# Start bytes of the matmul operands in SBUF: fixed tile strides, and odd weight chunks 128 bytes further on

## The reference

```python
        h = h + jax.nn.sigmoid(h @ w_ple_gate[i]) * e
...
        h = _layer_norm(DEEPNORM_ALPHA * h + mix, ln_g[layer, 0], ln_b[layer, 0])
        h = _layer_norm(DEEPNORM_ALPHA * h + _sq_relu_mlp(h, ffn_w1[layer], ffn_w2[layer]),
                        ln_g[layer, 1], ln_b[layer, 1])
```

## Time and profile before

| | |
|---|---|
| time, median of three runs | 1188.33 us (1186.57 to 1188.77) |
| span of the profiled execution | 1182.6 us |
| time around the span, against the median | 5.7 us |
| PE busy | 1134.0 us, 8737 matmuls |
| DVE busy | 822.2 us |
| ACT busy | 644.3 us |
| granted TensorE clock, mean | 0.978 |
| matmuls of `three` | 7860 |

### The profile page before, as it was taken

The page is one execution under the profiler, slowest core; times in us unless marked ns, Lnnn a source line. Parts: engine busy times, 40 slices in busy tenths (PEclk is TensorE's granted clock), DMA queues, the critical chain, the costliest instruction groups (busy, mean ns, idle before and its releaser), DMA issues.

```text
span 1182.6 us, 23980 instructions
## 1 busy us (share of the span) xinstructions
PE 1134.0 (96%) x8737; PEld 1077.7 (91%) x8737; DVE 822.2 (70%) x1454; ACT 644.3 (54%) x1249; POOL 412.5 (35%) x453
## 2 busy tenths in 40 slices
PE   6987989999998999999999999999999999999997
PEld 6975779999997989869999999999979999999996
DVE  6899688888557776755788745496456567887454
ACT  5675756555645555665556534374425645665342
POOL 5886332333413101124566412200013334665130
PEclk9998999999999999978999999999999999999998
DMA  6531156667455633303555555565422555555651
GB/s 191 139 116 36 37 143 172 184 182 200 135 195 187 205 119 96 113 31 108 171 160 173 178 174 177 172 217 180 164 72 85 198 180 174 182 177 183 199 175 48
DMA packets 199371, 178.27 MB, mean 151 GB/s; under 512 B 5730, under 2 KB 197589, under 8 KB 199044
## 3 DMA queue, kind: packets, MB, share of 16 engines
q1 hardware_dynamic: 198788, 173.37, 46.8%
q0 software_dynamic: 512, 3.96, 0.9%
HBM read 176.26 MB, written 1.05 MB: 150 GB/s over the span
## 4 chain that ended last, share of the span: by engine, by line
PE 80%; DVE 10%; ACT 4%; issue 2%; POOL 2%; DMA 1%; SPq 0%; ACTq 0%; DVEq 0%; POOLq 0%
PE ps L1799 24%; PE ps L1800 23%; PE ps L1801 23%; DVE wlo L1199 3%; PE ps L2147 2%; ACT whi L706 2%; DVE cv L1280 2%; PE ps L2277 2%; POOL acc L518 1%; PE ps L2104 1%; DVE ta L1412 1%; PE ps L2129 1%; PE ps L2255 1%; DMA raw<-w_in 1%; ACT sq L721 1%
## 5 line engine op out<-in xcount | busy, mean ns | idle before, releaser
L1199 DVE TENSOR_TENSOR wlo<-raw,whi 128x1024 fp32r<-128x1024 f32 x329 | 410.2, 1284 | 166.6 <-ACT whi L706 165.1
L706 ACT ACTIVATE whi<-raw 128x1024 fp32r<-128x1024 f32 x330 | 331.8, 1050 | 177.6 <-PE ps L1801 155.9
L1799 PE MATMUL ps<-xh,whi 128*128 128x256 f32 (+2 forms) x912 | 262.5, 288 | 13.8 <-DVE xl L1217 5.5
L1800 PE MATMUL ps<-xl,whi 128*128 128x256 f32 (+2 forms) x912 | 258.7, 284 | 0.0
L1801 PE MATMUL ps<-xh,wlo 128*128 128x256 f32 (+2 forms) x912 | 258.1, 283 | 0.0
L1799 PE MATMUL ps<-xrh,whi 128*128 128x274 f32 (+2 forms) x832 | 242.3, 291 | 0.0
L1801 PE MATMUL ps<-xrh,wlo 128*128 128x274 f32 (+2 forms) x832 | 238.7, 287 | 0.0
L1800 PE MATMUL ps<-xrl,whi 128*128 128x274 f32 (+2 forms) x832 | 238.6, 287 | 0.0
L1799 PE MATMUL ps<-fh,whi 128*128 128x256 f32 (+1 forms) x688 | 194.3, 282 | 1.9 <-DVE wlo L1199 1.9
L1800 PE MATMUL ps<-fl,whi 128*128 128x256 f32 (+1 forms) x688 | 194.5, 283 | 0.0
L1801 PE MATMUL ps<-fh,wlo 128*128 128x256 f32 (+1 forms) x688 | 193.9, 282 | 0.0
(11 more groups left out here) (327 smaller groups left out, 1694.7 us busy)
## 6 DMA issues: line engine op xcount, KB each, us to landing
raw<-ffn_w SPq DMA_DIRECT2D x128, 512.0 KB, 4.4
raw<-ret_w_in SPq DMA_DIRECT2D x48, 512.0 KB, 4.3
raw<-even_w_in SPq DMA_DIRECT2D x24, 512.0 KB, 4.7
raw<-w_ffn_gate SPq DMA_DIRECT2D x22, 512.0 KB, 4.1
raw<-w_ffn_up SPq DMA_DIRECT2D x22, 512.0 KB, 5.3
raw<-w_ffn_down SPq DMA_DIRECT2D x16, 512.0 KB, 4.4
raw<-ret_w_out SPq DMA_DIRECT2D x16, 512.0 KB, 4.4
raw<-w_in SPq DMA_DIRECT2D x12, 512.0 KB, 5.7
```

What stands on the lines that cost most here:

```text
L706: A(whi[:, slot, s * 1024:s * 1024 + 1024], raw[:, slot, s * 1024:s * 1024 + 1024], ACT.Copy).then_inc(w_hi_ready, 1)
L1199: V.tensor_tensor(wlo[:, slot, s * 1024:s * 1024 + 1024], raw[:, slot, s * 1024:s * 1024 + 1024], f32(whi[:, slot, s * 1024:s * 1024 + 102 ...
L1799: T.matmul(dst, w[0], x[0], start=first, stop=False)
L1800: T.matmul(dst, w[0], x[1], start=False, stop=False)
```

## The change

It moves operands to other start bytes and changes no instruction count. Slots of `whi` and `wlo` become 2080 columns long, so that slot 1 begins 128 bytes further in a line than slot 0. A pad of 48 columns stands before `xh`. `xh`, `xl`, `xrh`, `xrl` get a tile stride of 320 columns (1280 bytes). For the 256-column stages the same memory of `xh`, `fh`, `gh` (and their low parts) is read and written through views with a stride of 1024 bytes (`x1h`, `f1h`, `g1h`); those of `fh` and `gh` begin 16 columns in. `fh` and `fl` keep 1088 bytes in ffn_down0. The reserve for the descriptors of the POOL queue's DMAs falls from 16,384 to 8192 bytes. All writers and readers of the 256-column stages are changed to the views; the diff is cut to one of each kind.

```diff
+XS, WS = 320, CH + 32
...
-        whi = sb("whi", [P, 2, CH], F32R)
-        wlo = sb("wlo", [P, 2, CH], F32R)
-        xh = sb("xh", [P, KD, N2], F32R)
-        xl = sb("xl", [P, KD, N2], F32R)
+        whi = sb("whi", [P, 2, WS], F32R)
+        wlo = sb("wlo", [P, 2, WS], F32R)
+        sb("x_lines", [P, 48])
+        xh_mem = sb("xh", [P, KD, XS], F32R)
+        xl_mem = sb("xl", [P, KD, XS], F32R)
+        xh, xl = xh_mem[:, :, 0:N2], xl_mem[:, :, 0:N2]
+
+        def short_rows(t, depth, skip=0):
+            flat = t[:, :, :].rearrange("p k n -> p (k n)")
+            return flat[:, skip:skip + depth * N1].rearrange("p (k n) -> p k n", k=depth)
+
+        x1h, x1l = short_rows(xh_mem, KD), short_rows(xl_mem, KD)
...
         fh = f1("fh", [P, FT2, N2], F32R)
         fl = f1("fl", [P, FT2, N2], F32R)
+        f1h, f1l = short_rows(fh, FT2, META), short_rows(fl, FT2, META)
...
-        xrh = f1("xrh", [P, KD, N2 + 2], F32R)
-        xrl = f1("xrl", [P, KD, N2 + 2], F32R)
+        xrh = f1("xrh", [P, KD, XS], F32R)[:, :, 0:N2 + 2]
+        xrl = f1("xrl", [P, KD, XS], F32R)[:, :, 0:N2 + 2]
...
+        g1h, g1l = short_rows(gh, 16, META), short_rows(gl, 16, META)
...
-                A(xh[:, k, 0:N1], h[:, k, META:], ACT.Copy, scale=c1("g_ffn_pre", k)).then_inc(xh_ready, 1)
+                A(x1h[:, k, :], h[:, k, META:], ACT.Copy, scale=c1("g_ffn_pre", k)).then_inc(xh_ready, 1)
...
-            outputs("gate_up", FT // 2, TOK1, rows_x, x_from(X_FFN), gv_scaled, lambda j: j + 1, behind=lambda: stat(S_PRE))
+            outputs("gate_up", FT // 2, TOK1, rows_x1, x_from(X_FFN), gv_scaled, lambda j: j + 1, behind=lambda: stat(S_PRE))
...
-            outputs_deep("ret_out", S_LN + 2, LAST, rows_g, 16, lambda k: pe.wait_ge(y_ready, k + 1), behind=lambda: pe.wait_ge(silu2_ready, 16))
-            mlp(2, 1, X_LN2, FT2 // 2 + 8, FT + FT2, LAST)
+            outputs_deep("ret_out", S_LN + 2, TOK1, rows_g1, 16, lambda k: pe.wait_ge(y_ready, k + 1), behind=lambda: pe.wait_ge(silu2_ready, 16))
+            mlp(2, 1, X_LN2, FT2 // 2 + 8, FT + FT2, LAST, rows_f1, TOK1)
...
-    nc = bacc.Bacc("TRN2", target_bir_lowering=False, num_devices=1)
+    nc = bacc.Bacc("TRN2", target_bir_lowering=False, num_devices=1, dynamic_dma_scratch_size=8192)
```

More of the change, by code:

```diff
@@ L637, in _, with hidden @@
             forget_low(1)
-            def hidden(base, cols):
+            def hidden(base, cols, hi, lo):
                 def low(m, slot):
                     pool.wait_ge(f_hi, base + m + 1)
-                    nc.gpsimd.tensor_tensor(fl[:, at(m), cols], fa[:, slot, cols], f32(fh[:, at(m), cols]), ALU.subtract).then_inc(f_ready, 1)
+                    nc.gpsimd.tensor_tensor(lo[:, at(m), :], fa[:, slot, cols], f32(hi[:, at(m), :]), ALU.subtract).then_inc(f_ready, 1)
                 def turn(i):
@@ L659, in _ @@
             sums(S_LN, y, ALL)
-            hidden(FT, ALL)
+            hidden(FT, ALL, fh, fl)
             sums(S_LN + 1, y, ALL)
@@ L913, in gated_high @@
                 act.wait_ge(f_mul, m + 1)
-                A(fh[:, at(m), 0:N1], fa[:, u, 0:N1], ACT.Copy).then_inc(f_hi, 1)
+                A(f1h[:, at(m), :], fa[:, u, 0:N1], ACT.Copy).then_inc(f_hi, 1)
             def gelu(i):
@@ L1083, in residual, with ffn_up @@
                     split_at(C0[name] + per * i + per - 1 + 2)
-            def ffn_up(name, base, j, cols):
+            def ffn_up(name, base, j, cols, hi):
                 def turn(i):
@@ L1104, in high @@
                     act.wait_ge(f_mul, base + t + 1)
-                    A(fh[:, at(t), cols], fa[:, slot, cols], ACT.Copy).then_inc(f_hi, 1)
+                    A(hi[:, at(t), :], fa[:, slot, cols], ACT.Copy).then_inc(f_hi, 1)
                 repeat(act, 8, turn)
@@ L1111, in _ @@
             residual(S_LN, "even_out", 1, 0, ALL)
-            ffn_up("ffn_up0", FT, 0, ALL)
+            ffn_up("ffn_up0", FT, 0, ALL, fh)
             residual(S_LN + 1, "ffn_down0", 4, 1, ALL)
@@ L1167, in ret_gate @@
                         act.wait_ge(y_mul, t + 1)
-                        A(gh[:, at(t), LAST], fa[:, 2 * u + m, LAST], ACT.Copy).then_inc(y_hi, 1)
+                        A(g1h[:, at(t), :], fa[:, 2 * u + m, LAST], ACT.Copy).then_inc(y_hi, 1)
             repeat(act, 4, ret_gate)
@@ L1172, in _ @@
             residual(S_LN + 2, "ret_out", 2, 2, LAST)
-            ffn_up("ffn_up1", FT + FT2, 2, LAST)
+            ffn_up("ffn_up1", FT + FT2, 2, LAST, f1h)
             residual(S_LN + 3, "ffn_down1", 4, 3, LAST)
@@ L1700, in _ @@
                 for k in RET_TILES[c - 1] if c else ():
-                    x_low(X_RET, k, h[:, k, :], cols=ALL)
+                    x_low(X_RET, k, h[:, k, :], dst=(xh, xl), cols=ALL)
             def ret_value_tiles(j, u):
@@ L1794, in _ @@
             T = nc.tensor
-            rows_x, rows_q, rows_r, rows_f, rows_g = (xh, xl), (qxh, qxl), (xrh, xrl), (fh, fl), (gh, gl)
+            rows_x, rows_q, rows_r, rows_f = (xh, xl), (qxh, qxl), (xrh, xrl), (fh, fl)
+            rows_x1, rows_f1, rows_g1 = (x1h, x1l), (f1h, f1l), (g1h, g1l)
             def three(dst, w, x, first, last):
@@ L2063, in _ @@
                     c = C0["down"] + 3 * j + q
-                    product(c, c % 2, pair("down", j, N1), rows_f, TOK1, 256, kt=kt, k0=8 * q, first=q == 0, last=q == 2,
+                    product(c, c % 2, pair("down", j, N1), rows_f1, TOK1, 256, kt=kt, k0=8 * q, first=q == 0, last=q == 2,
                             ready=f_from(0) if j == 0 else None).then_inc(mm_done, 1)
```

36 lines of the change are left out of this document (18 added, 18 removed).

## The result

The changed kernel takes 1177.33 us, median of four runs (1177.1 to 1180.84), against 1188.19 for the kernel before (four runs, 1186.57 to 1188.77): ratio 0.9926, 95% interval 0.9913 to 0.9940. It is faster by 0.7%.

A forecast was written before the change was run, and what follows sets the result against it. PE bounds the kernel, its long stages being streams of back-to-back matmuls. Terms -11.8 - 5.2 - 0.6 + 0 + 0.3 + 1.0 = -16.3 us take the span from 1182.6 to 1166.3, plus 5.7 gives 1172.0; range 1166 to 1189.

The forecast's parts named there:

- 256 columns: Streams on x1, f1 and g1 rows, 3456 matmuls: start distance from 117.0 to 113.6 ns, -11.8 us.
- 258 columns: ffn_up1 and half of ret_qk, 960 matmuls on xrh: start distance from 120.4 to 115.0 ns, -5.2 us.
- lower bound of 114.2: Least start distance in ns allowed for the 258-column matmuls, where 115.0 was taken and 120.4 was the upper bound.
- 272 and 274 columns: Stages of these widths on xh and xrh: -0.6 us for xh, 0 and +0.3 us for xrh.
- xh at ALL: even_out and ret_v, 272 columns, 576 matmuls: start distance from 125.0 to 124.0 ns, -0.6 us.
- xrh: 274 columns, 960 matmuls: no change, 0; 272 columns (even_dqk and eight interleaved chunks), 576: 126.5 to 127.0 ns, +0.3 us.
- ret_g: 384 matmuls moved to 128 bytes into a line: start distance from 117.0 to 119.5 ns, +1.0 us.
- ffn_down0: 768 matmuls on fh, phases unchanged: 125.0 ns in any case, 0 us; a move would mean the weights' start byte counts.
- Rival 1: All streams: the relation of both start addresses counts, so at 256 columns only even chunks gain; -7.0 us, 1181.3 us; chance 0.27.
- w0 doing as w128: Odd 256-column chunks: weights at a line's start settle at 113.6 ns like those 128 bytes in, one whole moving line away.
- Rival 3: All streams: nothing happens, shorter groups are paid back by longer ones within a fixed period; 1188.3 us, within 2; chance 0.12.
- 5.7 us around the span: Whole kernel: difference between profiled span 1182.6 and median 1188.3 us, added to the forecast span 1166.3 to give 1172.0.

The follow-up runs named there:

- m1: Kernel without the computation: 57 streams of matmuls alone at chosen start bytes, other engines idle; eight repeats of one pair gave 113.3 ns (five) and 117.8 (three).
- e1: Changed kernel with slots of 2048 columns, so without the odd-chunk shift of the weights: 1178.78 us, ratio 0.9939.
- e2: Kernel before with only the slots of whi and wlo lengthened to 2080 columns, row tiles as before: 1187.64 us, ratio 1.0016.
- e4: Built on e1, no shift, with other fixed start bytes for the row tiles (x1 and g1 at 0, f1 at 192, xrh at 128): 1189.87 us beside 1185.47 before.
- e8: Changed kernel with xrh and xrl 64 bytes further on and no odd shift from even_dqk until the third chunk of ret_g: 1177.97 us, ratio 0.9919.
- e7: The changed kernel run again unaltered, against the kernel before: 1178.67 us, ratio 0.9926.
- e5: Changed kernel without the odd shift and with xrh and xrl 64 bytes further on: 1179.8 us, ratio 0.9928.
- e6: Changed kernel with xrh and xrl 64 bytes further on and, by a reversed condition, the odd shift only from even_dqk to ret_v: 1182.06 us, ratio 0.9951.

## Why the prediction was right, and where it was not

**256 columns: right, at 10.1 of 11.8 us.** From the table of stages: gate_up 3.84, down 1.07, ffn_down1 2.80, ret_out 1.16, qkv_in 0.30, conv_in 0.29, mix_out 0.50, ple_gate 0.17. The 113 ns read from four matmuls in the earlier trace rows is the settled rate, 113.3. What is missing was lost in chunks that settle at 117.8 instead, which the forecast didn't know of.

**258 columns: wrong, 0.4 us instead of 5.2.** This is the term that failed; it makes up 4.8 of the 6.4 us between the forecast's 16.3 and the 9.9 that the rates come to. It took the x64 rate of 256 columns and added two columns' time, 0.8 ns. In its place the runs show that each width has rates of its own: at x64 beside w128, 256 columns go at 113.3 and 258 at 120.8 (m1). Even the sign was wrong: e1, with the row tiles alone, has ffn_up1 at 120.85 against 120.3 before, and e2, with the shift alone, has 119.95. The 0.4 us of the change come from the odd chunks at w0 (118.9), on which the term did not rest. The best that any run has for 258 is 118.7; the lower bound of 114.2 was not reached anywhere. The earlier trace rows had an honest hint: ffn_up1's 120.4 was 3.4 above 117.0 for two columns, where the columns explain 0.8.

**272 and 274 columns: small, as predicted.** xh at ALL won nothing instead of 0.6: even chunks went to 123.4 as the earlier trace rows promised, odd ones to 126.6, and the shift took what the row tiles gave; e1 without it has 123.4 in both. xrh gave 0.3 us in ffn_up0 and 0.3 in the stages with 272, against 0 and +0.3, inside the bounds; e2, with the shift alone, gave the same in ffn_up0.

**ret_g: +0.84 against +1.0.** The size was right partly by luck: it came from ple, which is at x0 and goes at 118.65 once settled (e4), while ret_g is at x128, whose 119.85 and 118.6 happen to lie near.

**ffn_down0: +0.4 against 0.** The prediction called it 125.0 in any case and named what a move would mean; e2, where only the weights moved, shows the same 125.55, so it is the weights' start byte.

**Rival 1 was right in its mechanism and wrong in its price.** The relation counts: m1, and the two levels of even and odd chunks in even_out (123.4 / 126.6), ffn_up1 (120.8 / 118.9) and ret_g (119.85 / 118.6), each match a cell of its table within 0.2 ns. Elsewhere they don't: e8 has 120.0 / 122.1 in ffn_up1, where the cells of m1 have 120.8 and 120.0. And rival 1 priced odd chunks at 117.8 as x192 beside w128 is. That is one of the rates of that relation; the stream that comes in at 113.3 keeps it there. The forecast's reason for w0 doing as w128 (a shift of one whole moving line in time) doesn't hold as stated: x64 beside w0 by itself ran at 117.8 in m1. It held by what the stream brought along.

**Rival 3** is out: shorter groups were not paid back in gate_up, ret_out or ffn_down1.

**From rates to the span.** By rates the terms come to 10.1 + 0.4 + 0.3 + 0.3 - 0.84 - 0.4 = 9.9 us; the span fell by 7.3. Of the 2.6 between them 1.5 lie in attention behind the last chunk of even_v1, where the change touches no stream of `three`. Another 0.6 lie in down, whose pauses grew by as much, 0.3 in the first two stages and 0.2 in gate_up. Windows of qkv_in, conv_in and that part of attention: before, then after; the column behind POOL's count is the granted clock.

```profile
13.35:35.21 21.86, 20.96 (x164) 20.40 (x165) 18.22 (x37) 12.25 (x22) 18.17 (x22) 0.92 0.56 147
35.21:61.40 26.19, 25.32 (x207) 24.81 (x205) 20.93 (x37) 16.09 (x25) 18.92 (x21) 1.00 0.49 130
501.70:536.83 35.13, 35.13 (x199) 23.43 (x197) 16.81 (x79) 23.09 (x106) 6.90 (x12) 0.76 0.10 31
```

```profile
13.30:36.34 23.04, 22.06 (x165) 21.64 (x165) 18.74 (x37) 12.26 (x22) 19.33 (x23) 0.85 0.54 143
36.34:61.12 24.78, 24.78 (x207) 24.43 (x205) 20.55 (x37) 16.09 (x25) 17.52 (x20) 1.00 0.51 134
496.25:532.88 36.63, 36.63 (x200) 24.38 (x198) 16.57 (x79) 23.08 (x106) 6.89 (x12) 0.71 0.09 30
```

In attention PE is busy throughout, with the same matmuls, and takes 1.5 us more at a granted clock of 0.71 instead of 0.76. It follows the clock: the same part takes 35.8 to 37.1 us in the executions of e1 to e8, the longer the more of it is at 1.2 GHz, and 35.3 in the profile of before. Whether before is always so short is not known, as it has one profile. qkv_in too had a stretch at 1.2 GHz that before didn't have and took 1.2 us more, but conv_in behind it took 1.4 us less, since its last chunk no longer began behind a pause of 1.1 us. In e7, the same kernel, qkv_in takes 21.7 us instead of 23.0, and q begins at 61.2 in both.

**The 5.7 us around the span were mis-sized.** In every other execution of the two blocks, time and span differ by 1.8 us. The remaining 3.9 are best explained by the profiled execution of before, whose own time is not on record, having been that much faster than the median. So the span's 7.3 us understate the gain: between medians it is 10.9 us (1188.19 to 1177.33), against the 9.9 that the rates account for and the 16.3 predicted.

**What the shift is for: it releases slow streams.** Count the steps from an odd chunk to the even one behind it at 256 columns and x64, with no pause near them, at which the stream comes in slow. In the three kernels with the shift (change, e7, e8), where this is a step from w0 to w128, 13 of 17 went over to 113.3. In the three without it (e1, e5, e6), where all is at w128, 0 of 44 did; there a slow stream became fast only behind a pause, as in e1 at chunk 6 behind one of 1.5 us and in e6 at chunk 41 behind one of 2.1. At steps from an even chunk to an odd one it was 1 of 12 with the shift, the one shown in e8, and no fast stream became slow at any step. In the profiled executions without the shift gate_up or ffn_down1 is slow from end to end (but for gate_up's first chunk, which has pauses) four times out of six, with it never in six.

**It also has a cost at entries.** ret_out follows ret_g without a pause; its first chunk, 125, came in slow at w0 in all three kernels with the shift and fast at w128 in all three without. The two entries of down behind pauses, chunks 41 and 43, were slow in all three with the shift and in one of the three without.

**In times it is worth about 3 us.** The change and e1 alone don't separate (0.9926, 0.9913 to 0.9940, and 0.9939, 0.9922 to 0.9955). Taken together, the 16 executions of the three kernels without the shift lie at 0.9948 of their kernels before in the mean and the 14 with it at 0.9920: 3.3 us, 95% interval 1.8 to 4.8 by drawing the executions anew. The kernels differ in other stages too, but by their rates these differences cancel between the two groups to 0.2 us. The spreads (8.0, 6.4 and 6.5 us without, 3.7, 2.6 and 1.5 with) point the same way but show little by themselves: the kernel before spreads over 4.5 us in 13 executions and e2 over 6.0 in ten. How a stream comes to enter slow or fast was not found out beyond this: in m1 the same code did both.

## What to carry to other kernels

When PE is the bound and its matmuls follow without a pause, read the distance between starts by stage and by position in SBUF; a fixed start byte can be better or worse than a walking one (113.3 to 120.0 ns around 117.0 here), so measure each width by a stream of its own before building on it, and never carry a rate over to another width, even one of two columns more. When a stage has one rate in one execution and another in the next, look at single chunks: a mean over a stream that can hold two rates looks like noise. And price each part of an edit by itself: here the tiles brought most of the gain at 256 columns and a loss at 258, and the shift of the weights kept streams from staying slow, at a cost in stages that didn't need it.

## What the runs showed of the hardware that was not expected

- A stream of matmuls with fixed start bytes mostly settles within six to twelve matmuls into an exact period and keeps it over hundreds: 256 columns at 113.33 or 117.78 ns (x64 beside w128), 118.65 (x0), 120.0 (x128). Which of two it takes is settled at its entry; by what was not found out.
- A step of the weights' start byte from w0 to w128 took slow streams at x64 to the fast period (twice in m1, and at 13 of 17 unbroken steps in the kernels, such as chunks 125 to 126 of the change, 17 to 18 of e7 and 151 to 152 of e8). A step from w128 to w0 did so once in 12 (chunks 10 to 11 of e8).
- Two more columns can cost 7.5 ns (113.3 to 120.8) or, by another start byte, 0.9 (117.8 to 118.7 at x64 beside w0).
- All of it stands with the other engines and the DMA queues at rest (m1). The Trainium skill, page "SBUF — State Buffer", section "Who interferes with whom", says that PE never waits on anyone; nothing here contradicts that of other engines. But it gives no reason for start bytes to matter, and they change the distance by 6.7 ns. By its page "TensorE: Matmul & The Clock Gate", section "Back-to-back issue gap", the estimate for 256 columns is 109.2 ns; no stream in any run came under 113.3. The forecast left out that the section gives this formula for an isolated matmul and says that in a stream of weight loads and matmuls both set the spacing, so these runs are no test of it.
